# Relative-bias tables: the 0/1 masks of the bucket distances on VectorE replaced by signs that ScalarE makes during the projections

## The reference, cut to what matters

```python
rel = pos[q] - pos[k]                       # k in the block of q or the block before
def t5_bucket(rel):                         # 32 buckets
    n = jnp.maximum(rel, 0)
    large = 16 + (log(max(n, 1) / 16) / log(8) * 16).astype(int32)
    return jnp.where(n < 16, n, jnp.minimum(large, 31))
bias = rel_table[t5_bucket(rel)]            # one column of 32 values for each of 6 heads
s = jnp.where(mask, s + bias, -inf)
```

## Time and profile before

| | us |
|---|---|
| median of 3 runs | 4225.49 (4222.82 to 4228.16) |
| the profiled execution | 4221.91 |
| its span | 4220.1 |
| TensorE busy | 3874.7 (92%) |
| VectorE busy | 1993.7 (47%) |
| ScalarE busy | 1400.6 (33%) |
| GpSimd busy | 1524.3 (36%) |
| mean granted TensorE clock | 0.951 of full speed |

### The profile page before, as it was taken

One profiled execution on the slowest core, in us unless ns is written; L12 is line 12 of the kernel. 1 busy time (PEld: TensorE's weight loads), 2 busy tenths in 40 slices (PEclk: granted clock), 3 DMA queues, 4 the chain that ended last, 5 costly groups with the idle time before them and its releaser, 6 DMA issues. The chain is left out here.

```text
span 4220.1 us, 51879 instructions
## 1 busy us (share of the span) xinstructions
PE 3874.7 (92%) x19016; PEld 3022.0 (72%) x19016; DVE 1993.7 (47%) x3503; ACT 1400.6 (33%) x2168; POOL 1524.3 (36%) x738
## 2 busy tenths in 40 slices
PE   6978899999788889999999779899999998879999
PEld 5866688888566668876887643688878876437887
DVE  3786866443646676654454854322232231452222
ACT  3244322222326443333223253322232233433222
POOL 1330143444130135553544310455545443104454
PEclk9989999999989999999999877999999999779999
DMA  7611144432110136653663210233323332102232
GB/s 241 187 36 30 44 140 131 148 105 64 32 38 1 38 107 220 214 167 129 226 226 119 65 40 1 60 95 94 96 83 95 94 86 67 34 1 79 91 97 78
DMA packets 460357, 411.40 MB, mean 97 GB/s; under 512 B 28080, under 2 KB 405296, under 8 KB 460208
## 3 DMA queue, kind: packets, MB, share of 16 engines
q1 hardware_dynamic: 457759, 408.11, 31.3%
q10 hardware_dynamic: 2448, 1.32, 0.1%
HBM read 405.71 MB, written 7.60 MB: 98 GB/s over the span
## 5 line engine op out<-in xcount | busy, mean ns | idle before, releaser
L212 POOL TENSOR_TENSOR s_wlo<-s_raw,s_whi 128x1024 fp32r<-128x1024 f32 x490 | 1181.2, 2418 | 2112.5 <-ACT s_whi L204 2112.0
L226 PE MATMUL psum<-s_xhi,s_whi 128*128 128x512 f32 x3264 | 1230.3, 377 | 52.7 <-DVE s_t L391 19.8
L227 PE MATMUL psum<-s_xlo,s_whi 128*128 128x512 f32 x3264 | 1222.9, 375 | 0.0
L228 PE MATMUL psum<-s_xhi,s_wlo 128*128 128x512 f32 x3264 | 1218.0, 373 | 0.0
L204 ACT ACTIVATE s_whi<-s_raw 128x1024 fp32r<-128x1024 f32 x490 | 510.6, 1057 | 1827.4 <-PE psum L228 1822.6
L226 PEld LDWEIGHTS psum<-s_xhi,s_whi 128*128 128x128 f32 x3264 | 617.0, 189 | 175.0 <-issue 53.5
L227 PEld LDWEIGHTS psum<-s_xlo,s_whi 128*128 128x128 f32 x3264 | 616.8, 189 | 112.3 <-issue 4.6
L228 PEld LDWEIGHTS psum<-s_xhi,s_wlo 128*128 128x128 f32 x3264 | 616.0, 189 | 111.8
L226 PE MATMUL psum<-s_ahi,s_whi 128*128 128x512 f32 x1232 | 476.6, 387 | 10.8 <-DVE s_y L1128 7.1
L228 PE MATMUL psum<-s_ahi,s_wlo 128*128 128x512 f32 x1232 | 469.7, 381 | 0.0
L227 PE MATMUL psum<-s_alo,s_whi 128*128 128x512 f32 x1232 | 469.5, 381 | 0.0
(11 more groups left out here) (263 smaller groups left out, 4174.8 us busy)
## 6 DMA issues: line engine op xcount, KB each, us to landing
s_ada_raw<-w_ada SPq DMA_DIRECT2D x224, 512.0 KB, 3.8
s_raw<-w_gu SPq DMA_DIRECT2D x176, 512.0 KB, 3.8
s_raw<-w_up SPq DMA_DIRECT2D x88, 512.0 KB, 4.8
s_raw<-w_dn SPq DMA_DIRECT2D x88, 512.0 KB, 3.5
s_raw<-w_down SPq DMA_DIRECT2D x44, 512.0 KB, 4.4
s_raw<-w_in SPq DMA_DIRECT2D x30, 512.0 KB, 3.9
s_raw<-w_in_ab SPq DMA_DIRECT2D x20, 512.0 KB, 6.3
s_area<-w_first SPq DMA_DIRECT2D x16, 512.0 KB, 11.8
```

Source lines behind the costliest of these rows:

```text
L212: pool.tensor_tensor(K.wlo[:, c % HL, 0:a * b], K.raw[:, c % RAW, 0:a * b], K.whi[:, c % HL, 0:a * b].bitcast(F32), ALU.subtract).then_inc ...
L226: pe.matmul(out, lh, rh, start=first, stop=False)
L227: pe.matmul(out, lh, rl, start=False, stop=False)
L228: return pe.matmul(out, ll, rh, start=False, stop=last)
```

## The change

The mask is 0 or 1; the sign of (distance - least + 0.5) is -1 or +1. The table is then the mean of the first and the last bucket's value plus the sum over the buckets of half a step times the sign, which is the same sum. ScalarE makes the 31 signs (`activation` with function Sign and a bias column for each bucket, from a new block `least` of the column table) into two buffers of 512 in `t2`, alternately. VectorE only adds, and the masks go. A sign waits until the adds of the bucket two before are done (`sign_used`), an add until its sign is there (`sign_ready`), and the first sign until the distances are (`rel_ready`). In ScalarE's order the signs stand in the projection given as `during`, in batches of about equal size ahead of the products 1 to the last: each batch before that product's `split_hi` and eviction. VectorE's order stays; the first table's phase now stands behind its projection in the list.

```diff
@@ Proj.act
         for i, ((_, n, _, read), tok, own) in enumerate(self.products):
+            if self.table:
+                self.table.signs(e, *(31 * max(j, 0) // (len(self.products) - 1) for j in (i - 1, i)))
             if tok is None:
@@ BiasTable
-    def __init__(self, K, heads, tables):
+    def __init__(self, K, heads, tables, during):
+        during.table = self
...
-        return {"bias_ready": 1}
+        return {"bias_ready": 1, "rel_ready": 1, "sign_ready": 31, "sign_used": 31}
+
+    def sign(self, b):
+        a = TX + b % 2 * TX
+        return self.K.t2[:, :, :].rearrange("p a t -> p (a t)")[:, a:a + TX]
+
+    def signs(self, e, first, end):
+        K = self.K
+        for b in range(first, end):
+            if b == 0:
+                e.wait_ge(self.sem["rel_ready"], self.at("rel_ready", 1))
+            if b >= 2:
+                e.wait_ge(self.sem["sign_used"], self.at("sign_used", b - 1))
+            c = COLS["least"] + b
+            e.activation(self.sign(b), K.t2[:, 0, 0:TX], ACT.Sign, bias=K.cols[:, c:c + 1]).then_inc(self.sem["sign_ready"], 1)
...
         e.tensor_tensor(delta, tab[:, :, 1:32], tab[:, :, 0:31], ALU.subtract)
+        e.tensor_tensor(mean, tab[:, :, 0], tab[:, :, 31], ALU.add)
...
+        e.tensor_scalar(delta, delta, 0.5, None, ALU.mult)
+        e.tensor_scalar(mean, mean, 0.5, None, ALU.mult)
...
-            ins = e.tensor_scalar(self.sums[i], rel, 0.0, tab[:, h, 0:1], ALU.mult, ALU.add)
+            ins = e.tensor_scalar(self.sums[i], rel, 0.0, mean[:, h:h + 1], ALU.mult, ALU.add)
...
-        for b, least in list(enumerate(self.least()))[1:]:
-            e.tensor_scalar(mask, rel, float(least), None, ALU.is_ge).then_inc(K.sem["dve_step"], 1)
-            e.wait_ge(K.sem["dve_step"], K.step())
+        for b in range(31):
+            e.wait_ge(self.sem["sign_ready"], self.at("sign_ready", b + 1))
             for i, h in enumerate(self.heads):
-                ins = e.scalar_tensor_tensor(out=acc[i], in0=mask, scalar=K.b_delta[:, h, b - 1:b], in1=acc[i],
-                                             op0=ALU.mult, op1=ALU.add)
-            ins.then_inc(K.sem["dve_step"], 1)
-            e.wait_ge(K.sem["dve_step"], K.step())
+                ins = e.scalar_tensor_tensor(out=self.sums[i], in0=self.sign(b), scalar=K.b_delta[:, h, b:b + 1],
+                                             in1=self.sums[i], op0=ALU.mult, op1=ALU.add)
+            ins.then_inc(self.sem["sign_used"], 1)
+            e.wait_ge(self.sem["sign_used"], self.at("sign_used", b + 1))
@@ build
-        table = BiasTable(K, [0], first_table)
+        v = proj(T0, w_in, [(2048 + g * 256, 256, True, tokens_to(K.vtok, g * 256)) for g in range(2)])
+        table = BiasTable(K, [0], first_table, v)
...
-        w_out(T0, io["w_out_ab"], mixed)
-        BiasTable(K, [1, 2], b_acc)
+        BiasTable(K, [1, 2], b_acc, w_out(T0, io["w_out_ab"], mixed))
...
-        BiasTable(K, [3], b_acc)
+        BiasTable(K, [3], b_acc, w_out(TX, io["w_out_c"], mixed))
...
-            proj(TX, w, jobs, x_ready)
+            ph = proj(TX, w, jobs, x_ready)
             if l == 0:
-                BiasTable(K, [4, 5], b_acc)
+                BiasTable(K, [4, 5], b_acc, ph)
```

More of the change, by code:

```diff
@@ L735, in __init__ @@
     def __init__(self, K, T, w, jobs, x_wait=None, tasks=(), gate=None):
-        self.T, self.x_wait, self.gate, self.norm, self.pool_first = T, x_wait, gate, None, None
+        self.T, self.x_wait, self.gate, self.norm, self.pool_first, self.table = T, x_wait, gate, None, None, None
         self.half = T // P // 2
@@ L1860, in distances @@
         rel, own = K.t2[:, 0, 0:TX], K.t2[:, 1, 0:TX]
-        posf, posq, tab, delta = self.posf, K.b_posq, K.b_tab, K.b_delta
+        posf, posq, tab, delta, mean = self.posf, K.b_posq, K.b_tab, K.b_delta, K.b_mean
         e.tensor_copy(posf, self.pos[:, :])
@@ L1878, in distances @@
         e.wait_ge(K.sem["dve_step"], K.step())
-        e.tensor_tensor(rel, rel, own, ALU.add).then_inc(K.sem["dve_step"], 1)
-        e.wait_ge(K.sem["dve_step"], K.step())
+        e.tensor_tensor(rel, rel, own, ALU.add).then_inc(self.sem["rel_ready"], 1)
+        e.wait_ge(self.sem["rel_ready"], self.at("rel_ready", 1))
         for i, h in enumerate(self.heads):
-            ins = e.tensor_scalar(self.sums[i], rel, 0.0, tab[:, h, 0:1], ALU.mult, ALU.add)
+            ins = e.tensor_scalar(self.sums[i], rel, 0.0, mean[:, h:h + 1], ALU.mult, ALU.add)
         ins.then_inc(K.sem["dve_step"], 1)
         e.wait_ge(K.sem["dve_step"], K.step())
[L1886 to L1891, removed]
     def dve(self, e):
@@ L1897, in dve @@
         self.distances(e)
-        rel, mask, acc = K.t2[:, 0, 0:TX], K.t2[:, 1, 0:TX], self.sums
-        for b, least in list(enumerate(self.least()))[1:]:
-            e.tensor_scalar(mask, rel, float(least), None, ALU.is_ge).then_inc(K.sem["dve_step"], 1)
-            e.wait_ge(K.sem["dve_step"], K.step())
+        for b in range(31):
+            e.wait_ge(self.sem["sign_ready"], self.at("sign_ready", b + 1))
             for i, h in enumerate(self.heads):
-                ins = e.scalar_tensor_tensor(out=acc[i], in0=mask, scalar=K.b_delta[:, h, b - 1:b], in1=acc[i],
-                                             op0=ALU.mult, op1=ALU.add)
-            ins.then_inc(K.sem["dve_step"], 1)
-            e.wait_ge(K.sem["dve_step"], K.step())
-        for table, total in zip(self.tables, acc):
+                ins = e.scalar_tensor_tensor(out=self.sums[i], in0=self.sign(b), scalar=K.b_delta[:, h, b:b + 1],
+                                             in1=self.sums[i], op0=ALU.mult, op1=ALU.add)
+            ins.then_inc(self.sem["sign_used"], 1)
+            e.wait_ge(self.sem["sign_used"], self.at("sign_used", b + 1))
+        for table, total in zip(self.tables, self.sums):
             ins = e.tensor_copy(table, total)
@@ L2345, in build @@
         K.b_posq, K.posq_i = K.small[:, 378:382], K.small[:, 382:386].bitcast(I32)
-        sinks = K.small[:, 386:398]
+        sinks, K.b_mean = K.small[:, 386:398], K.small[:, 398:404]
         with ExitStack() as ffn:
@@ L2732, in lay_out @@
         out_norm=col(on.reshape(-1)), conv=np.concatenate(conv, 1), freq=freq)
+    d = np.arange(129)
+    large = 16 + (np.log(np.maximum(d, 1) / 16).astype(f) / f(np.log(8)) * 16).astype(int)
+    bucket = np.where(d < 16, d, np.minimum(large, 31))
+    parts_["least"] = np.tile(0.5 - np.array([np.argmax(bucket >= b) for b in range(1, 32)], f), (P, 1))
     cols = np.zeros((P, NCOL), f)
```

7 lines of the change are left out of this document (3 added, 4 removed).

## The result

| | median, us | lowest to highest | ratio to before |
|---|---|---|---|
| before (4 runs beside it) | 4226.07 | 4222.82 to 4228.16 | |
| after (4 runs) | 4192.92 | 4189.02 to 4196.07 | 0.9923 [0.9907, 0.9939] |

The change makes the kernel 33.15 us faster; forecast were 24.9, and 4201 us. The interval of the ratio is some 26 to 39 us. The profiled execution of after took 4196.07 us (span 4194.3), the slowest of its four, and the profiled one of before 4221.91 us, less than any of its timed runs, so the two traces lie only 25.8 us apart. In the traces I compare the start of the k-th matmul in both ("aligned"), and how far this difference moves over a stretch; all traces hold the same 19016 matmuls. Stretches are given by the times of before: the first table's place is 206 to 272 us (up to the second step of the attention behind it), the third's 1450 to 1545, the fourth's 2316 to 2416.

The account below looks back on a forecast made before the run. TensorE was busy 92% of the span, so only its waits for VectorE's four tables could shrink. Gains of 7.0 + 0 + 4.8 + 13.1 = 24.9 us gave a median of 4201 us, range 4186 to 4216.

Parts of the forecast that it names:

- three late VectorE ends of 10.5, 5.9 and 20.6 us: First, third and fourth tables: VectorE's table ends the wait last, so up to 37.0 us could be recovered.
- Costs of a Sign and a hand-over: ScalarE: 0.73 us a Sign, 0.66 behind another, hand-over 0.04 each way; buckets of 0.80 (one head) or 1.45 us (two).
- no table load for Sign: Rival: Sign needs its own table load, felt in first and fourth tables, 2.6 us less gain, 4203 us; chance 0.08.
- First table, 7.0 us: Projection and attention behind the first table: 9.5 us earlier maximum less 2.5 for GpSimd, between 2 and 10.5 us.
- earlier maximum: First table: the attention's first maximum at 253.2 instead of 262.73 us, 9.5 us earlier.
- minus 2.5: First attention: three or four scalings meet GpSimd's work and lose about one us each, some off the chain.
- Second table, 0: Second table's projection: five Signs take 5.7 us and fit the 6.64 us gap, so no gain or loss.
- Third, 4.8: Third table: VectorE's lateness of 5.9 us behind rstd goes, less 1.1 us; range 3 to 5.9 us.
- Fourth, 13.1: Fourth table: 20.6 us of VectorE's lateness goes, less 7.5 for a new TensorE stall and slow clock; range 8 to 20.6.
- 30 more columns in the first load: taken as nothing: Column table: the columns added to the first load come before anything that waits for them and cost no time.
- Full recovery: Rival: all three waits of VectorE go and nothing takes their place, 37.0 us, 4188 us; chance 0.12.
- The slower rival's price, 60q: Rival: q us more a bucket costs about 60q; from q = 0.56 slower by 0.2% (4234 us); chance 0.05.

Follow-up runs that it names:

- only_first: Signs made for the first table only, masks kept in the other three, larger column table kept, against before: 4212.92 us, ratio 0.9977.
- pad_only: The kernel before, all instructions kept, its column table widened by 30 unused columns so that later buffers start 120 bytes later: 4215.84 us, ratio 0.9984.
- only_third: Signs made for the third table only, masks kept in the other three, larger column table kept, against before: 4211.09 us, ratio 0.9973.
- only_fourth: Signs made for the fourth table only, masks kept in the other three, larger column table kept, against before: 4198.43 us, ratio 0.9948.
- sign_twice: The changed kernel with every Sign made twice, the second waiting for the first by a semaphore: 4234.22 us, ratio 1.0027 to before.
- pad_eight: The kernel before with its column table widened by 8 unused columns, so that later buffers start 32 bytes later: 4206.01 us in one execution.
- late4: The changed kernel with the fourth table's Signs two products later, none before product 3: 4186.23 us, ratio 0.9917 to before.
- after_pad: The changed kernel with 2 more unused columns, so that later buffers start 128 bytes later than in before, not 120: 4194.48 us, ratio 0.9939 to before.

## Why the prediction was right, and where it was not

- What bounds, and three late VectorE ends of 10.5, 5.9 and 20.6 us: right. Behind the tables VectorE now waits for TensorE or ScalarE, or follows it within 0.1 us.
- Costs of a Sign and a hand-over (0.73, 0.66, 0.80 a bucket, 1.45 with two heads): right to 0.02 us; no table load for Sign (35 loads in both traces), which ends that rival in this kernel. Batches of 10 and 11 took 8.0 and 8.8 us for 7.8 and 8.6.
- First table, 7.0 us: measured 3.0 by the medians, and up to the attention's second step 2.3 in the trace of after and 7.8 in that of only_first. The term "earlier maximum" is 7.7, not 9.5: the last eviction was 1.1 us and the scores another 0.8 later, beside a clock that gave 5.49 us for the 16 matmuls that took 4.50. The mis-sized term is "minus 2.5" for GpSimd. I took the longest stretch of before, 2.25 us, as the bound for one instruction. There each instruction of VectorE had waited for one of GpSimd's and no more, and the masks beside this very run took 1.12 us for 0.43. The scaling missed two gaps and lost 5.4 us. Behind it the attention gives back 3.1 us more (272 to 398 us), at a granted clock of 0.88 against 0.94 in before; pad_only, whose instructions are those of before, loses 3.3 there, so this is not the Signs' doing. My sum had no term for it.
- Second table, 0: right; it measured -1.8, within what the medians of 11 runs scatter.
- Third, 4.8: measured 4.9 by the medians; aligned 3.9 in after and 5.2 in only_third, the difference being the clock in the norm behind it.
- Fourth, 13.1: measured 17.5 by the medians; aligned 14.0 in after. In relation to the wait of the earlier trace rows (8.36 us earlier in after) I put the distances at 2319.8, and they ended at 2319.31; piece 5 whole at 2329.8, and it was at 2329.25; the stall at 5.5, and it was 5.02. only_fourth's own trace gives 17.0 at this place: it loses 6.8 where after loses 8.0, and gets 23.7 back where after gets 22.0, at a granted clock of 1.00 from 2345 to 2416 us where after had 0.97.
- The Trainium skill's rule on the port pair (SBUF — State Buffer, "SBUF: two separate sides") was used for the distances, and the trace agrees there: the three lines behind GpSimd's piece took 0.69 us each, and one scaling beside it 2.47. The same section calls the pair an exclusive lock for a whole instruction. The 5.99 us are the rest of three instructions of GpSimd's (1.8 to 2.1 us each), which that rule did not make me expect.
- "30 more columns in the first load: taken as nothing": wrong by 6 to 7 us. Without the layout the change gives 33.15 - 7.2 = 26 us, where my sum gave 24.9. That this is so close is partly luck: by the medians one term is too large by 4 and one too small by about as much, both within their scatter. With the layout the gain stands a hair outside the forecast's own band (17 to 33 us, 4193 to 4209), and by its number alone 4192.92 is nearer to the rival "Full recovery" (4188); the traces decide against that one, since the stall of 5.02 us and the stretched scaling are there.
- The whole, aligned: the places of the tables give 2.3 + 3.9 + 14.0 = 20.2 us, the six stretches of the Ffn 10.4, and stretches at another granted clock take back 2.7 (60 to 120 us, 0.92 against 0.97), 3.1 (the first attention) and 1.9 (2416 to 2660 us, 0.77 against 0.79). That makes 22.9 of the 25.8 us between the two traces; the rest is spread over what lies between.
- The slower rival's price, 60q: sign_twice has q = 0.57 us, for which I had worked out 34 us more, and against after it was 41.3. The mechanism is right and its price within a fifth; it needs a Sign that costs twice what it does.

## What to carry to other kernels

When a faster engine reaches its next work earlier, look at what that work will now run beside: here GpSimd's back-to-back instructions took most of the first table's gain in the trace of after, and a wait in the right place gave it back. A batch that waits on another engine should go into a queue behind the work that a third engine needs next, not ahead of it. And a change that allocates anything moves every buffer behind it: run the kernel before with that padding alone before the gain is put down to the edit.

## What the runs showed of the hardware that was not expected

- The start of the buffers in SBUF changes the pace of the fp32r matmuls of 128x512 that read `ahi` and `alo`: 226.7 to 233.4 ns from one to the next with the same instructions at a granted clock of 1.00, 10 us over six stretches of this kernel from before to after, 17.6 to pad_eight. The Trainium skill (SBUF — State Buffer, "SBUF: two separate sides") says that within the engine side only the shared port pair causes contention, so that TensorE waits for nobody; that alone does not account for these rows.
- A VectorE scaling of 128x768 from SBUF to SBUF, 0.62 us alone, took 5.93 to 5.99 us in three kernels (after, late4, sign_twice) beside three GpSimd instructions in a row, 1.83 to 1.84 in two others (after_pad, only_first) in which it stood at nearly the same place of the same run, and 0.62 where GpSimd waited for it.
- The same attention work (2480 to 2660 us of before) took 182.3 us at a granted clock of 0.75 in after and 176.4 at 0.79 in after_pad, one trace of each; before took 180.0 at 0.76 and late4 182.0 at 0.77, so the clock of the stretch alone does not give its time.
